# Two plain product groups at the head of each feed-forward block

## The reference, cut to what matters

```python
x = x + jnp.square(jax.nn.relu(h2 @ w_up[l])) @ w_down[l]            # first block, D_FF = 4096
def swiglu(h, w_gate, w_up, w_down):                                  # D_FF_2 = 2816
    return (jax.nn.silu(h @ w_gate) * (h @ w_up)) @ w_down
x = x + 0.5 * swiglu(rms_norm_2(x, ffn1_norm[l]), ffn1_wg[l], ffn1_wu[l], ffn1_wd[l])
```

## Time and profile before

| what | us |
|---|---|
| median of 3 runs | 2599.92 |
| lowest, highest | 2599.77, 2603.3 |
| the profiled execution | 2600.92 |
| its span (first to last instruction) | 2599.1 |
| TensorE busy | 2457.6 |
| VectorE busy | 1871.0 |
| ScalarE busy | 1296.5 |
| GpSimd busy | 193.6 |

### The profile page before, as it was taken

The page is one execution under the profiler, slowest core; times in us unless marked ns, Lnnn a source line. Parts: engine busy times, 40 slices in busy tenths (PEclk is TensorE's granted clock), DMA queues, the critical chain, the costliest instruction groups (busy, mean ns, idle before and its releaser), DMA issues.

```text
span 2599.1 us, 37586 instructions
## 1 busy us (share of the span) xinstructions
PE 2457.6 (95%) x14980; PEld 2191.9 (84%) x14980; DVE 1871.0 (72%) x2744; ACT 1296.5 (50%) x2103; POOL 193.6 (7%) x199
## 2 busy tenths in 40 slices
PE   9999969999978999999879999799999998799999
PEld 7878858999868999978679999689999787699998
DVE  6742566777769878666678878788877666788775
ACT  6676344444454444357454444545444474544444
POOL 2221010000030000012100000100000121000001
PEclk9999989999989999999989999899999999899999
DMA  7655322333312333235323333223332363133331
GB/s 201 144 130 129 116 88 81 99 105 98 106 57 81 99 106 98 73 112 140 97 65 106 98 98 99 81 85 102 98 98 82 105 154 97 57 98 98 101 111 66
DMA packets 103646, 263.83 MB, mean 102 GB/s; under 512 B 9648, under 2 KB 12976, under 8 KB 103088
## 3 DMA queue, kind: packets, MB, share of 16 engines
q1 hardware_dynamic: 94848, 233.57, 28.9%
q0 software_dynamic: 8624, 27.86, 5.3%
HBM read 234.56 MB, written 2.19 MB: 91 GB/s over the span
## 4 chain that ended last, share of the span: by engine, by line
PE 69%; DVE 15%; ACT 6%; issue 6%; DMA 3%; POOL 1%; SPq 0%; POOLq 0%; DVEq 0%; ACTq 0%
PE bank L1058 11%; PE bank L1059 11%; PE bank L1060 11%; PE bank L1086 11%; PE bank L1087 11%; PE bank L1088 11%; DVE slot_lo L1527 2%; ACT w_hi L1246 2%; DVE x L1782 1%; DVE h_mixed L1557 1%; DVE w_raw_lo L1527 1%; PE bank L1102 1%; PE bank L1117 1%; DMA w_raw<-w_out_dram 1%; DVE slot_raw L1579 1%
## 5 line engine op out<-in xcount | busy, mean ns | idle before, releaser
L1086 PE MATMUL bank<-h_hi,slot_hi 128*128 128x256 f32 x1664 | 481.8, 290 | 59.7 <-DVE h_lo L1527 44.6
L1088 PE MATMUL bank<-h_hi,slot_lo 128*128 128x256 f32 x1664 | 476.5, 286 | 0.0
L1087 PE MATMUL bank<-h_lo,slot_hi 128*128 128x256 f32 x1664 | 476.5, 286 | 0.0
L1291 ACT ACTIVATE slot_hi<-slot_raw 128x1024 fp32r<-128x1024 f32 (+1 forms) x416 | 381.4, 946 | 173.9 <-DVE slot_raw L1579 144.3
L1527 DVE TENSOR_TENSOR slot_lo<-slot_raw,slot_hi 128x1024 fp32r<-128x1024 f32 (+1 forms) x416 | 441.4, 1083 | 0.0
L1058 PE MATMUL bank<-act_hi,w_hi 128*128 128x512 f32 x960 | 382.8, 399 | 17.8 <-DVE w_raw_lo L1527 17.3
L1086 PEld LDWEIGHTS bank<-h_hi,slot_hi 128*128 128x128 f32 x1664 | 323.1, 194 | 83.2 <-DVE h_lo L1527 47.2
L1059 PE MATMUL bank<-act_lo,w_hi 128*128 128x512 f32 x960 | 381.8, 398 | 0.0
L1060 PE MATMUL bank<-act_hi,w_raw_lo 128*128 128x512 f32 x960 | 376.3, 392 | 0.0
L1086 PE MATMUL bank<-hs_hi,slot_hi 128*128 128x256 f32 x1248 | 356.5, 286 | 15.0 <-ACT part_b L1306 7.9
L1306 ACT ACTIVATE part_a<-bank 128x256 f32<-128x256 f32 x208 | 79.3, 381 | 555.0 <-PE bank L1088 532.9
(11 more groups left out here) (252 smaller groups left out, 4150.4 us busy)
## 6 DMA issues: line engine op xcount, KB each, us to landing
slot_raw<-ffn_wg_dram SPq DMA_DIRECT2D x88, 512.0 KB, 3.9
slot_raw<-ffn_wu_dram SPq DMA_DIRECT2D x88, 512.0 KB, 3.8
w_raw<-ffn_wd_dram SPq DMA_DIRECT2D x88, 512.0 KB, 3.6
w_raw<-w_in_dram SPq DMA_DIRECT2D x67, 512.0 KB, 3.7
w_lo<-w_raw POOLq DMA_DIRECT2D x43, 512.0 KB, 5.1
slot_raw<-w_up_dram SPq DMA_DIRECT2D x32, 512.0 KB, 4.1
w_raw<-w_down_dram SPq DMA_DIRECT2D x32, 512.0 KB, 3.6
w_raw<-w_out_dram SPq DMA_DIRECT2D x24, 512.0 KB, 3.6
```

Source lines behind the costliest of these rows:

```text
L1086: engine.matmul(to, slot_hi[:, g % 2, slot, lhs], hi, start=opens, stop=False, skip_group_check=True)
L1087: engine.matmul(to, slot_hi[:, g % 2, slot, lhs], lo, start=False, stop=False, skip_group_check=True)
L1088: product = engine.matmul(to, slot_lo[:, g % 2, slot, lhs], hi, start=False, stop=closes, skip_group_check=True)
L1291: engine.activation(span_of(slot_hi, n, name), span_of(slot_raw, n, name), ACT.Copy).then_inc(signals["s_hi"].s, 1)
```

## The change

The first two groups of every feed-forward block (for stage 1 its first two pairs, for the others the first gate and the first up group) become plain products: eight steps over each of the two hidden tiles with 512 columns, 48 products in all, the last two steps of both tiles at the end. They need the weights without sums, and h without mixed quarters. Tiles of h are made by `h_tile` as in the mixers, ScalarE's high part and one VectorE instruction for the low part. The quarters are made by jobs of their own (`mix_full`, `mix`, `mix_hi`, `mix_lo`): those of the first pair of tiles four slots after tile 1, the other three beside the first plain group, at its slots 2, 8 and 14. The norm's sum, root and reciprocal come 1, 3 and 6 slots after step 11 of that group (stage 2 keeps its own form). In the output projections a unit is split 6 slots after its fetch, not 1, and its low part two slots after the high part. `FF_RING` goes from 10 to 8; hs_lo gets room of its own, and h_full now lies where part_a and part_b are.

```diff
-FF_RING = 10
+FF_RING = 8
+PLAIN_PARTS = {"plain_a": (B11, 2), "plain_b": (B22, 2)}
+PLAIN_SLOT = ((B11, B21), (B12, B22))
-OPENING = ("P1", "P2", "P4", "P6", "P7", "P5", "P3")
+LEAD = 2
...
     def norm(self, s):
+        if s in MLP_STAGES and s != 2:
+            self.later(1, "norm_sum", s)
+            self.later(3, "norm_root", s)
+            self.later(6, "norm_inv", s)
+            return
...
     def norm_tile(self, s, m):
-        self.add("hs_tile" if s in MLP_STAGES else "h_tile", (s, m))
+        self.add("h_tile", (s, m))
         self.square(s, m)
-        if s in MLP_STAGES and m % 2 == 1:
-            self.add("h_mix", (s, m // 2))
-            self.later(2, "h_mix_lo", s, m // 2)
+        if s in MLP_STAGES and m == 1:
+            self.mix(s, 0, 4)
...
+    def mix(self, s, j, slots):
+        self.later(slots, "mix_full", s, j)
+        self.later(slots + 2, "mix", s, j)
+        self.later(slots + 5, "mix_hi", s, j)
+        self.later(slots + 7, "mix_lo", s, j)
...
     def out_projection(self, source, s):
         self.block_first[s] = len(self.results)
+        self.split_job = "split_late"
         n = self.begin_block(s)
         for m in range(KT):
-            self.residual(m, self.dense(KT, 0, source))
+            self.residual(m, self.dense(KT, 0, source, slots=6))
...
+        if self.sg[n].plain:
+            steps = ((0, "s_hi", (n, "plain_a")), (2, "s_hi", (n, "plain_b")), (2, "s_lo", (n, "plain_a")), (4, "s_lo", (n, "plain_b")))
...
+    def plain(self, g):
+        group = self.sg[g]
+        order = [(n, k) for n in range(2) for k in range(KT - 2)] + [(n, k) for n in range(2) for k in (KT - 2, KT - 1)]
+        if self.pending_norm is not None:
+            for j in range(1, HALF_K):
+                self.mix(group.stage, j, 6 * (j - 1) + 2)
+        for at, (n, k) in enumerate(order):
+            if at == 11 and self.pending_norm is not None:
+                self.norm(self.pending_norm)
+                self.pending_norm = None
+            if k == KT - 1:
+                self.add("p_last", (g, n))
+            else:
+                self.add("p_step", (g, n, k))
+            self.next_slot()
...
+                    engine.matmul(to, slot_hi[:, g % 2, slot, lhs], h_hi[:, k, :], start=k == 0, stop=False)
+                    engine.matmul(to, slot_hi[:, g % 2, slot, lhs], h_lo[:, k, :], start=False, stop=False)
+                    product = engine.matmul(to, slot_lo[:, g % 2, slot, lhs], h_hi[:, k, :], start=False, stop=job == "p_last")
...
+                elif job == "mix_full":
+                    s, j = key
+                    act.wait_ge(*x_is(s, 2 * j))
+                    act.wait_ge(*x_is(s, 2 * j + 1))
+                    act.wait_ge(*done(*h_until[s]))
+                    if s - 1 in MLP_STAGES:
+                        act.wait_ge(*done("s_out", h_until[s][1][0]))
+                    if j > 0:
+                        act.wait_ge(*done("mix_4", (s, j - 1)))
+                    engine.activation(h_full[:, 0, :], x[:, 2 * j, :], ACT.Copy, scale=h_gain(s, 2 * j))
+                    engine.activation(h_full[:, 1, :], x[:, 2 * j + 1, :], ACT.Copy, scale=h_gain(s, 2 * j + 1)).then_inc(signals["mix_full"].s, 1)
...
-                elif job == "h_mix":
+                elif job == "mix":
                     s, j = key
-                    v.wait_ge(*done("h_full", (s, 2 * j + 1)))
+                    v.wait_ge(*done("mix_full", key))
                     if j > 0:
-                        v.wait_ge(*done("mix_hi", (s, j - 1)))
+                        v.wait_ge(*done("mix_lo", (s, j - 1)))
```

More of the change, by code:

```diff
@@ L143 @@
     order: tuple
-    opens: bool
+    plain: bool
 class Plan:
@@ L167 @@
         "s_load_a": (), "s_load_b": (),
-        "hs_tile": ("h_full", "h_hi", "h_lo"), "h_mix": ("mix_31", "mix_2", "mix_4", "mix_hi"), "h_mix_lo": ("mix_lo",),
+        "mix_full": ("mix_full",), "mix": ("mix_31", "mix_2", "mix_4"), "mix_hi": ("mix_hi",), "mix_lo": ("mix_lo",),
         "neg_rms": ("neg_rms",),
@@ L533, in begin_block @@
             for kind, pair in kinds:
-                opens = pair == 0 and kind != "up"
-                self.sg.append(Group(stage, kind, pair, OPENING if opens else STEADY, opens))
+                self.sg.append(Group(stage, kind, pair, STEADY, pair * len(set(kind for kind, _ in kinds)) < LEAD))
         self.block_end = len(self.sg)
@@ L547, in prepare @@
         self.prepared += 1
[L548 to L550 removed]
+        if self.sg[n].plain:
+            steps = ((0, "s_hi", (n, "plain_a")), (2, "s_hi", (n, "plain_b")), (2, "s_lo", (n, "plain_a")), (4, "s_lo", (n, "plain_b")))
+        else:
+            steps = ((0, "s_t13", (n,)), (1, "s_t2", (n,)), (1, "s_hi", (n, "first")), (2, "s_t4", (n,)),
+                     (2, "s_hi", (n, "last")), (3, "s_lo", (n, "first")), (4, "s_hi", (n, "mixed")), (5, "s_lo", (n, "last")),
+                     (6, "s_hi", (n, "b21")), (7, "s_lo", (n, "mixed")), (9, "s_lo", (n, "b21")))
+        for after, job, key in steps:
             self.later(slots + after, job, *key)
@@ L575, in strassen @@
             self.prepare(g + 1)
+        if group.plain:
+            self.plain(g)
+            return
         quota, passed = self.quota, 0
@@ L892, in group_source, with strassen_before @@
             return dram[f"{ffn}_{'wg' if group.kind == 'gate' else 'wu'}"][0 if group.stage < 5 else 1, group.pair]
+        def strassen_before(g):
+            return max((n for n in range(g) if not plan.sg[n].plain), default=None)
         def zs_of(g):
@@ L988, in two_blocks @@
                 x_of["now", key] = r
-            elif job in ("h_tile", "hs_tile", "square", "square_first", "square_last", "output_gain", "output_gain_last") and key[0] > 0:
+            elif job in ("h_tile", "square", "square_first", "square_last", "output_gain", "output_gain_last") and key[0] > 0:
                 x_of[key] = x_of["now", key[1]]
@@ L1913, in two_blocks @@
                 project_buffer[key] = zs
+            elif job == "norm_root":
+                root_buffer[key] = zs
             elif job == "rescale":
```

195 lines of the change are left out of this document (112 added, 83 removed).

## The result

The changed kernel takes 2503.53 us (median of 4 runs, 2501.46 to 2504.8); the kernel before, run beside it, 2599.85 (4 runs, 2599.33 to 2603.3). The ratio is 0.9626, with a 95% interval of 0.9609 to 0.9643. Predicted were 2510 us, in a range of 2470 to 2543. The profiled execution took 2501.46 us (span 2499.3), 99.5 less than that of before (2600.92).

The account below looks back on a forecast made before the run. TensorE's work bounds the kernel, plus its waits and halved clock, some 160 us at five borders. Tails 51.1 plus openings 39.9 gain 91.0 us: 2600.92 to 2509.9, predicted 2510, range 2470 to 2543.

Parts of the forecast that it names:

- Tails of stages 1, 4 and 7: Last eight result tiles before these feed-forward blocks: free of waits, 35.1 us gained.
- Tails of stages 2 and 5: Last eight result tiles before these blocks: still 8 us lost in stage 2 and 3 in stage 5.
- Openings: First two groups of each block: 22.2 us each, 88.8 us gained if nothing is late behind them.
- The third group's wait: Behind each opening TensorE waits for slot_lo, VectorE's queue being late: five waits, 35.9 us, plus 13 of clock.
- Rival 1: The third group of each block is in time, so the openings keep their full gain: 2461 us; chance 0.18.
- rival 4: The waits only move from the border to the third group at full size, without gain: 2600 us; chance 0.02.
- The mix at 0.69 and not 1.76: VectorE's first mix instruction takes 0.69 us outside stage 2, as 1.76 came from GpSimd additions; otherwise chains some 2.5 longer.
- rival 2: Mixes stay at 1.76 us (12.5 us) and tails of stages 2 and 5 lose as before (16): 2538; chance 0.27.
- The half clock and the short waits: Work at the lower clock behind the third groups' waits loses 2, 2, 2, 3 and 4 us, 13 in all.
- The units split later: Output projections' weight units split six slots later: margin 4.3 us, cost 0, from a gain of 1 us down.
- rival 3: Units in the output projections come too late and TensorE waits in every one: slower, 2647 us; chance 0.02.
- The ring: Act tiles, 8 instead of 10: cost 0; 1 us each if a ScalarE wait came in each of 22 chunks.

Follow-up runs that it names:

- a_add_small: The changed kernel with GpSimd's additions of both square sums in stage 2 cut to 64 of 512 columns (values not the reference's): 2498.7 us, ratio 0.9608.
- b_square_behind: The kernel before, with the square of every odd tile issued behind the mix of its pair: 2583.3 us, ratio 0.9943.
- b_ring_8: The kernel before with a ring of 8 act tiles instead of 10, nothing else: 2598.51 us, ratio 1.0003.
- a_norm_block: The changed kernel with the norm's root, reciprocal and negation issued at once, in their place, as before the change: 2502.35 us, ratio 0.9633.

## Why the prediction was right, by its steps

**Tails of stages 1, 4 and 7: right.** Free of waits was expected, 35.1 us gained; they lose nothing at all now, and gained 11.78 + 11.68 + 11.76 = 35.2. The windows of the earlier trace rows are not the eight tiles that the prediction calls the tail (they hold 4.5 tiles in these stages, 12 and 9.5 in stages 2 and 5); over the last seven tiles the loss before was 60.0 us, not 62.1. That, and not what was left of the loss, makes the tails' gain 2.2 us smaller than forecast.

**Tails of stages 2 and 5: the sum right, each size off by 2.** Expected to lose were 8 and 3 us; against 84 x 0.2267 = 19.04 they lose 6.0 and 5.0. That GpSimd's additions cause stage 2's is shown by a_add_small: with short additions its tail takes 20.90 us, not 25.06. Whether by what they cost VectorE or by the z buffers that they hold, as the prediction had it, that run can't tell. Of stage 5's I had reckoned with VectorE being late but not with the half clock behind the one wait (3.09 us, then 3.4 at the lower level). Nor had I reckoned with GpSimd there: the prediction has it in the way in stage 2 alone. The page's row for the unit's low half, against the earlier trace rows, has a mean of 1336 ns, not 1280: 16 of these instructions now take 2.3 us, where 8 did, and four of the new ones are in stage 5, three of these ahead of its border.

```profile
L1600 DVE TENSOR_TENSOR w_raw_lo<-w_raw,w_hi 128x1024 fp32r<-128x1024 f32 x176 | 235.1, 1336 | 48.7 <-ACT w_hi L1315 48.4
```

The low half on which TensorE's wait of 3.09 us ends, at 1601.88, is one of them, started 0.11 us after an addition, and another (1590.40) went before it:

```profile
1599.43 1.31 POOL L2019 TENSOR_TENSOR square_sum<-square_sum,z 128x512 f32<-128x512 f32 x1 [3.43 <-ACT z L1303]
1599.54 2.29 DVE L1600 TENSOR_TENSOR w_raw_lo<-w_raw,w_hi 128x1024 fp32r<-128x1024 f32 x1
```

Each is 1.1 us longer than the usual 1.22, so up to 2.2 of the 3.09 us may be theirs; no run tests it.

**Openings: right.** An opening was expected at 22.2 us; it takes 22.38 of products (24.15 in stage 2, where 22.7 were expected: the two sums of its norm are of float32 without a split, and take 1.10 us each). TensorE's timeline in stage 2:

```profile
723.54 1.10 PE L1260 MATMUL bank<-scaled_sum,ones 128*128 128x512 f32 x2 [1.11 <-POOL scaled_sum L2019]
```

**The third group's wait: right in its mechanism and its sum, the step on which the forecast hung.** VectorE's chain at stage 4, where the border is at 1251.20, in the changed kernel:

```profile
1254.01 0.75 DVE L1617 SCALAR_TENSOR_TENSOR h_lo<-x,gains,h_hi 128x512 fp32r<-128x512 f32 x1 [0.79 <-ACT h_hi L1328]
1256.62 0.69 DVE L1600 TENSOR_TENSOR sum_lo<-square_sum,sum_hi 128x512 fp32r<-128x512 f32 x1 [1.85 <-ACT sum_hi L1423]
...
1266.54 0.43 DVE L1631 SCALAR_TENSOR_TENSOR h_mixed<-h_mixed,h_full 128x256 f32<-128x256 f32 x1
1267.26 3.35 DVE L1760 RECIPROCAL rms_inv<-z 128x512 f32<-128x512 f32 x1 [0.29 <-ACT z L1428]
...
1276.68 0.69 DVE L1660 TENSOR_TENSOR slot_raw<-slot_raw 128x512 f32<-128x512 f32 x1
1277.29 2.35 DVE L1600 TENSOR_TENSOR slot_lo<-slot_raw,slot_hi 128x1024 fp32r<-128x1024 f32 x2
```

From the border, predicted and measured: the norm's low half done at 5.4 and 6.1 us, the third mix at 14.5 and 15.8, the reciprocal at 18.4 and 19.4, TensorE's start at 26.3 and 27.4. Waits of 5.2, 14.5, 4.1, 8 and 4.1 us were expected in stages 1, 2, 4, 5 and 7; they are 6.43, 12.05 (and 2.2 for the norm's sums ahead of it), 4.99, 6.38 and 5.11: 35.0 in all, of 35.9. That the sum is so close is partly luck: three waits are 0.9 to 1.2 us longer than forecast, those of stages 2 and 5 are 2.4 and 1.6 us shorter. Rival 1 (the third group in time, 0.18) and rival 4 (waits of the old size, 0.02) fall with these rows.

**The mix at 0.69 and not 1.76: right,** shown by b_square_behind. In stage 2, where rival 2's condition holds, the price is paid by both engines. VectorE in the changed kernel:

```profile
698.78 1.35 DVE L1625 TENSOR_TENSOR h_mixed<-h_full 128x512 f32<-128x512 f32 x1 [1.61 <-ACT h_full L1340]
703.10 2.29 DVE L1600 TENSOR_TENSOR w_raw_lo<-w_raw,w_hi 128x1024 fp32r<-128x1024 f32 x1
```

and GpSimd:

```profile
698.28 1.30 POOL L2019 TENSOR_TENSOR scaled_sum<-scaled_sum,z 128x512 f32<-128x512 f32 x1
703.00 1.31 POOL L2019 TENSOR_TENSOR square_sum<-square_sum,z 128x512 f32<-128x512 f32 x1 [3.42 <-ACT z L1303]
704.28 2.25 POOL L2019 TENSOR_TENSOR scaled_sum<-scaled_sum,z 128x512 f32<-128x512 f32 x1
```

The low half that started 0.10 us after an addition takes 2.29 us, not 1.22, and ends 1.08 us after that addition; the addition that started meanwhile takes 2.25, not 1.30. The Trainium skill has the rule (SBUF — State Buffer, "Who interferes with whom": the first to issue keeps the shared pair of ports for its whole instruction, and the other blocks); the trace agrees, in both directions.

**The half clock and the short waits: the terms that were mis-sized.** 13 us were expected for the clock behind the third group's waits, and no change otherwise in the groups that follow. The windows view of TensorE over the four groups behind the opening of stage 4 (us, PE busy (x), PEclk, DMA share, GB/s), before and after:

```profile
1340.91:1391.46 50.55, 49.72 (x374) 1.00 0.31 94
```

```profile
1278.56:1329.55 50.99, 50.91 (x373) 0.96 0.28 84
```

Before, the granted clock is 1.00 in these windows of all five stages. After, it is 0.97, 0.95, 0.96, 0.97 and 0.95 in stages 1, 2, 4, 5 and 7. Twice the missing share of each window gives 4.6, 5.4, 4.1, 3.0 and 5.1 us at the lower level, 22.2 in all. What such a stretch costs is read from TensorE's timeline behind the wait of stage 4:

```profile
1279.15 0.41 PE L1157 MATMUL bank<-h_hi,slot_lo 128*128 128x256 f32 x1
...
1281.92 0.41 PE L1155 MATMUL bank<-hs_hi,slot_hi 128*128 128x256 f32 x1
```

These starts are 13 products apart, 0.213 us each, against 0.120 at the full clock: 1.78 times, not twice. So 0.44 of the 22.2 us are lost, an estimate of 9.7 us where 13 were forecast: about 2 each in stages 1, 4 and 7, as expected, but 2.4 and 1.3 in stages 2 and 5 instead of 4 and 3. The four groups take only 2.0 us more than before, though, so 7.7 us of something else are gone. I had not counted that. 4.7 of them are idle time of TensorE in these windows (6.95 us before, 2.27 after; part_b and slot_lo are what it waited for before); the rest is not taken apart.

**The units split later: wrong.** The step said cost 0, from a gain of 1 us down to rival 3. Taken out of the change, it costs 8 us; alone, it gives 15. I asked whether TensorE would get the unit in time, which it does, and not what it costs VectorE's queue when ScalarE waits for the landing: without the late split VectorE waits 2.0 to 3.2 us ahead of the first mix, and the third groups wait 8.48, 7.46 and 7.46 us in stages 1, 4 and 7 instead of 6.43, 4.99 and 5.11. The total is not wrong by it, since my chain already ran through the new order, with tile 7's residual and low half first behind the border. Rival 3 (units too late) is excluded by the tails.

**The ring, the norm's spread: right,** each within what can be measured (b_ring_8, a_norm_block).

**The sum.** From the forecast to the profiled execution, in us gained: tails -2.2, the openings' own products -2.2, their waits -1.2 (37.1 us, with the 2.2 of stage 2's sums, against 35.9); the clock +3.3, the short waits and what goes with them +7.7, elsewhere +3.0. In all the execution is 8.4 us under the 2509.9 that the sum gave, and short waits that end in the later groups, a gain that the prediction did not see, make up most of that.

## What to carry to other kernels

When work is moved away from a border, follow the helping engine's queue to its next consumer and add it up instruction by instruction: here that chain gave five waits of 35.9 us where 35.0 were found. Look in that queue for an instruction that nobody near needs (the second reciprocal of stage 2), for a copy that waits for a transfer with urgent work behind it (the units split early), and for an instruction that starts just behind another engine's addition: each of these moves was worth 4 to 15 us without a computation less. A step that costs TensorE nothing isn't worth nothing; ask what it frees on the engine that is late next.

## What the runs showed of the hardware

- A VectorE tensor_tensor of 512 float32 columns takes 0.68 to 0.69 us alone and 1.35 to 1.76 when it starts shortly after a GpSimd addition; one of 1024 goes from 1.22 to 2.3; the GpSimd addition itself, when it starts during such an instruction, from 1.30 to 2.25. To issue square and addition behind the mix instead of ahead of it gained 15 us of 2600.
- At the lower clock level a product of 256 columns takes 1.78 times as long (0.213 against 0.120 us), not twice, so that such a stretch costs 0.44 of its length.
- ScalarE's table load (1.28 us) was all that a change of function cost there: in the changed kernel the load that started at 1265.24 followed an instruction that ended by 1265.22, and the next began at 1266.54.
